# Two 64-step chunks as one 128-step unit in the HGRN2 recurrence, with the scaled state copies on ScalarE

## What is computed

```python
b = jnp.cumsum(log_f, axis=2)                       # within a chunk of 64
b_mid  = b[:, :, HG_CHUNK // 2 - 1:HG_CHUNK // 2]
b_last = b[:, :, HG_CHUNK - 1:HG_CHUNK]
scores = einsum('bnthk,bnshk->bnhts', q * exp(b - b_mid), k * exp(b_mid - b))
scores = where(causal, scores, 0.0)                 # 64 x 64
o_intra = einsum('bnhts,bnshv->bnthv', scores, iv)
q_dec, k_dec = q * exp(b), k * exp(b_last - b)
def step(state, xs):                                # one chunk after another
    o = einsum('bthk,bhkv->bthv', qc, state)
    state = dc[..., None] * state + einsum('bthk,bthv->bhkv', kc, ic)
```

## Time and profile before

| | |
|---|---|
| runs | 2416.03, 2418.9, 2420.78 us |
| median | 2418.9 us |
| span of the profiled execution, first to last instruction | 2413.7 us |
| mean granted TensorE clock | 0.979 |
| TensorE busy with matmuls | 2307.7 us (96%) |
| VectorE busy | 1268.4 us (53%) |
| ScalarE busy | 875.3 us (36%) |
| POOL busy | 146.6 us (6%) |

### The profile page before, as it was taken

One profiled execution on the slowest core, in us unless ns is written; L12 is line 12 of the kernel. 1 busy time (PEld: TensorE's weight loads), 2 busy tenths in 40 slices (PEclk: granted clock), 3 DMA queues, 4 the chain that ended last, 5 costly groups with the idle time before them and its releaser, 6 DMA issues. The chain is left out here.

```text
span 2413.7 us, 30798 instructions
## 1 busy us (share of the span) xinstructions
PE 2307.7 (96%) x11056; PEld 1867.0 (77%) x11056; DVE 1268.4 (53%) x2445; ACT 875.3 (36%) x1241; POOL 146.6 (6%) x255
## 2 busy tenths in 40 slices
PE   5899999999999999799999999979999999999997
PEld 2788888888888888688777777757877777778775
DVE  6454545454545544301556566555566565665655
ACT  6343333333333333111233323333343353354343
POOL 0000000000000000110111111110001000100100
PEclk9899999999999999899999999989999999999998
DMA  4100101010101010222222222165436535634622
GB/s 157 35 36 23 44 9 43 9 43 13 44 17 35 17 35 10 71 71 73 77 86 85 76 90 86 56 200 172 125 97 205 168 107 175 201 106 123 227 93 79
DMA packets 89269, 206.40 MB, mean 86 GB/s; under 512 B 20832, under 2 KB 30048, under 8 KB 89184
## 3 DMA queue, kind: packets, MB, share of 16 engines
q1 hardware_dynamic: 68432, 139.68, 18.3%
q0 software_dynamic: 20752, 65.57, 8.2%
HBM read 157.87 MB, written 46.14 MB: 85 GB/s over the span
## 5 line engine op out<-in xcount | busy, mean ns | idle before, releaser
L95 PE MATMUL s_ps<-u_hi,s_w_hi 128*128 128x512 f32 x768 | 305.8, 398 | 8.7 <-DVE s_w_lo L854 8.7
L96 PE MATMUL s_ps<-u_lo,s_w_hi 128*128 128x512 f32 x768 | 300.5, 391 | 0.0
L97 PE MATMUL s_ps<-u_hi,s_w_lo 128*128 128x512 f32 x768 | 299.8, 390 | 0.0
L95 PE MATMUL t_ps<-t_oa_hi,t_w_hi 128*128 128x512 f32 x512 | 204.6, 400 | 17.0 <-DVE t_oa_lo L1534 12.5
L97 PE MATMUL t_ps<-t_oa_hi,t_w_lo 128*128 128x512 f32 x512 | 202.4, 395 | 0.0
L96 PE MATMUL t_ps<-t_oa_lo,t_w_hi 128*128 128x512 f32 x512 | 202.3, 395 | 0.0
L1425 DVE TENSOR_TENSOR t_w_lo<-c_raw,t_w_hi 128x1024 fp32r<-128x1024 f32 x136 | 166.5, 1224 | 62.7 <-ACT t_w_hi L1331 62.7
L95 PEld LDWEIGHTS s_ps<-u_hi,s_w_hi 128*128 128x128 f32 x768 | 144.7, 188 | 53.1 <-issue 14.5
L97 PEld LDWEIGHTS s_ps<-u_hi,s_w_lo 128*128 128x128 f32 x768 | 144.8, 189 | 31.0
L96 PEld LDWEIGHTS s_ps<-u_lo,s_w_hi 128*128 128x128 f32 x768 | 144.8, 189 | 28.5
L1331 ACT ACTIVATE t_w_hi<-c_raw 128x1024 fp32r<-128x1024 f32 x136 | 142.5, 1048 | 42.4 <-PE t_ps L97 14.5
(11 more groups left out here) (277 smaller groups left out, 4794.3 us busy)
## 6 DMA issues: line engine op xcount, KB each, us to landing
c_raw<-w_in_in SPq DMA_DIRECT2D x56, 512.0 KB, 3.7
gates_scratch<-s_stage POOLq DMA_DIRECT2D x64, 256.0 KB, 2.7
t_ein<-gates_scratch SPq DMA_DIRECT2D x64, 256.0 KB, 4.2
c_raw<-w_o_hg_in SPq DMA_DIRECT2D x32, 512.0 KB, 5.0
c_raw<-w_out_in SPq DMA_DIRECT2D x32, 512.0 KB, 3.5
c_raw<-w_ple_gate_in SPq DMA_DIRECT2D x32, 512.0 KB, 3.5
c_raw<-w_glu_in SPq DMA_DIRECT2D x16, 512.0 KB, 3.9
t_xa<-o_gated_scratch POOLq DMA_DIRECT2D x32, 256.0 KB, 4.3
```

What stands on the lines that cost most here:

```text
L95: pe.matmul(out, w_hi, u_hi, start=first, stop=False)
L96: pe.matmul(out, w_hi, u_lo, start=False, stop=False)
L97: return pe.matmul(out, w_lo, u_hi, start=False, stop=last)
```

## The change

Two chunks of 64 steps become one unit of 128. Since a unit's scores now reach from its second half back to its first, keys and queries are kept in three forms of 64 columns a unit, ke[P, 4, 3, 64] and qe[P, 4, 3, 64]: for the keys the first half as seen from the middle of the first chunk (0), the same scaled by the decay up to the middle of the second (1), and the second half (2); for the queries the first half (0), the second as seen from the first chunk (1), and the second (2). The decay is the column coef of the second chunk. The scores of a unit are then two matmuls: 64 key columns (form 0) against 128 query columns (forms 0 and 1) into the upper 64 rows of psc, and 64 key columns (form 2) against 64 query columns (form 2) into the lower 64 rows. The lower left quarter is never written by them, so psc is set to zero once, and the mask is now the full triangle of 128.

The state is kept for 4 units instead of 8 chunks. VectorE makes G alone, with one fused instruction for a unit, and the scaled copies S come from ScalarE (`scale_states`), between the sigmoid L455 and the load of the table L456. G has two buffers. The span of a unit is the product of two coefficients and lies in R. The matrix of ones is made as F32R once and read as F32 where it was F32 (the rounded copy ones_r goes).

```diff
-            pool.wait_ge(mk, 5)
-            pool.memset(c["causal"][0:CH, CH:P], 0.0).then_inc(mk, 1)
...
-        qe = m.sb("qe", [P, TT])
-        ke = m.sb("ke", [P, TT])
+        qe = m.sb("qe", [P, NPAIR, 3, CH])
+        ke = m.sb("ke", [P, NPAIR, 3, CH])
-        S = m.sb("S", [P, NCH, P])
-        G = m.sb("G", [P, P])
+        S = m.sb("S", [P, NPAIR, P])
+        G = m.sb("G", [P, 2, P])
...
-                pe.wait_ge(qe_done, s + 1)
+                pe.wait_ge(q_far_done, s + 1)
+                pe.wait_ge(psc_zeroed, 1)
                 for p in range(NPAIR):
-                    pe.matmul(psc[:, at], ke[:, at], qe[:, at], start=True, stop=True).then_inc(turned, 1)
+                    near, both = slice(p * P + CH, (p + 1) * P), slice(p * P, (p + 1) * P)
+                    pe.matmul(psc[0:CH, both], ke[:, p, 0], qe[:, p, 0:2].rearrange("p a j -> p (a j)"), start=True, stop=True)
+                    pe.matmul(psc[CH:P, near], ke[:, p, 2], qe[:, p, 2], start=True, stop=True).then_inc(turned, 1)
 
             def outer(s):
-                for j in range(NCH):
-                    rows = slice(j % 2 * CH, j % 2 * CH + CH)
-                    out = (pk, pv)[j % 2][:, j // 2 * P:j // 2 * P + P]
-                    ins = pe.matmul(out, ken[rows, j // 2], ivn[rows, j // 2], start=True, stop=True)
+                for p in range(NPAIR):
+                    ins = pe.matmul(pk[:, p * P:(p + 1) * P], ken[:, p], ivn[:, p], start=True, stop=True)
...
             def attend(s, first):
                 for p in range(NPAIR):
-                    for j in (2 * p, 2 * p + 1):
-                        pe.wait_ge(states, s * NCH + j + 1)
-                        pe.matmul(po[:, at], S[:, j], qe[:, at], start=j % 2 == 0, stop=False, skip_group_check=True)
+                    pe.wait_ge(states, s * NPAIR + p + 1)
+                    pe.matmul(po[:, at], S[:, p], qe[:, p, 0:2].rearrange("p a j -> p (a j)"), start=True, stop=False,
+                              skip_group_check=True)
                     pe.matmul(po[:, at], ivn[:, p], sT[:, p], start=False, stop=True, skip_group_check=True).then_inc(o_done, 1)
...
+            def scale_states(s, new_head):
+                for p in range(1 if new_head else 0, NPAIR):
+                    act.wait_ge(g_done, s * NPAIR + p)
+                    act.activation(S[:, p], G[:, (p + 1) % 2], ACT.Copy, scale=coef[:, 2 * p:2 * p + 1]).then_inc(states, 1)
...
-                    dve.tensor_scalar(S[:, j], G[:], coef[:, j:j + 1], None, ALU.mult).then_inc(states, 1)
-                    dve.wait_ge(states, s * NCH + j + 1)
-                    dve.tensor_tensor(G[:], kv, S[:, j], ALU.add).then_inc(g_done, 1)
+                    dve.wait_ge(g_done, s * NPAIR + p)
+                    if p:
+                        dve.wait_ge(states, s * NPAIR + p)
+                    dve.scalar_tensor_tensor(G[:, p % 2], G[:, (p + 1) % 2], span[:, p:p + 1], kv, ALU.mult, ALU.add).then_inc(g_done, 1)
...
-                    dve.scalar_tensor_tensor(ke[:], sig[:], 1.0, b[:], ALU.subtract, ALU.mult).then_inc(ke_done, 1)
+                    dve.scalar_tensor_tensor(ke[:, :, 0], half(sig, 0), 1.0, half(b, 0), ALU.subtract, ALU.mult).then_inc(k_near_done, 1)
+                    dve.scalar_tensor_tensor(ke[:, :, 2], half(sig, 1), 1.0, half(b, 1), ALU.subtract, ALU.mult).then_inc(ke_done, 1)
+                    dve.tensor_tensor(ke[:, :, 1], ke[:, :, 0], second, ALU.mult).then_inc(k_far_done, 1)
+                    dve.tensor_tensor(span, coef[:, 0:NCH:2], coef[:, 1:NCH:2], ALU.mult).then_inc(span_done, 1)
...
-                    dve.scalar_tensor_tensor(qe[:], pq[:], c["nomlb"][:, ds(h, 1)], lf[:], ALU.mult, ALU.mult).then_inc(qe_done, 1)
+                    dve.scalar_tensor_tensor(qe[:, :, 2], half(pq, 1), c["nomlb"][:, ds(h, 1)], half(lf, 1), ALU.mult, ALU.mult
+                    dve.scalar_tensor_tensor(qe[:, :, 0], half(pq, 0), c["nomlb"][:, ds(h, 1)], half(lf, 0), ALU.mult, ALU.mult
+                    dve.tensor_tensor(qe[:, :, 1], qe[:, :, 2], second, ALU.mult).then_inc(q_far_done, 1)
...
+            dve.memset(psc[:], 0.0).then_inc(psc_zeroed, 1)
-            act.activation(ones_r[:], c["ones"][:], ACT.Copy).then_inc(ones_done, 1)
```

More of the change, by code:

```diff
@@ L152, in _ @@
         def _(pool):
-            pool.memset(c["ones"][:], 1.0).then_inc(ones_done, 1)
+            pool.memset(c["ones"][:].bitcast(F32), 1.0).then_inc(ones_done, 1)
             pool.memset(c["ident"][:], 0.0).then_inc(mk, 1)
@@ L172, in _ @@
                 pe.wait_ge(sq_done, n + 1)
-                pe.matmul(ms[:, t], c["ones"][:], sq[:, n % 2], start=k == 0, stop=k == KT - 1).then_inc(ms_done, 1)
+                pe.matmul(ms[:, t], c["ones"][:].bitcast(F32), sq[:, n % 2], start=k == 0, stop=k == KT - 1).then_inc(ms_done, 1)
         @block.scalar
@@ L480, in _ @@
             turned_iv(STEPS - 1)
+            scale_states(STEPS - 1, False)
             norm(STEPS - 1, False)
@@ L487, in _ @@
             chunks = lambda x: x[:].rearrange("p (n j) -> p n j", j=CH)
+            half = lambda x, i: x[:].rearrange("p (a b j) -> p a b j", b=2, j=CH)[:, :, i]
+            second = coef[:].rearrange("p (a b) -> p a b", b=2)[:, :, 1:2].to_broadcast([P, NPAIR, CH])
             col = lambda x: x.rearrange("p (n a) -> p n a", a=1)
@@ L499, in turned_scores, with carry_state @@
                                     psc[:].rearrange("p (a n) -> p a n", a=NPAIR)).then_inc(masked, 1)
-            def carry_state(s, new_head):
+            def carry_state(s, new_head, first):
                 dve.wait_ge(kv_done, s + 1)
-                for j in range(NCH):
-                    kv = (pk, pv)[j % 2][:, j // 2 * P:j // 2 * P + P]
-                    if new_head and j == 0:
+                dve.wait_ge(span_done, s + 1)
+                if not first:
+                    dve.wait_ge(states, s * NPAIR)
+                for p in range(NPAIR):
+                    kv = pk[:, p * P:(p + 1) * P]
+                    if new_head and p == 0:
                         dve.memset(S[:, 0], 0.0).then_inc(states, 1)
-                        dve.wait_ge(states, s * NCH + 1)
-                        dve.tensor_copy(G[:], kv).then_inc(g_done, 1)
+                        dve.tensor_copy(G[:, 0], kv).then_inc(g_done, 1)
                         continue
-                    if j == 0:
-                        dve.wait_ge(coef_done, s + 1)
-                    dve.wait_ge(g_done, s * NCH + j)
-                    dve.tensor_scalar(S[:, j], G[:], coef[:, j:j + 1], None, ALU.mult).then_inc(states, 1)
-                    dve.wait_ge(states, s * NCH + j + 1)
-                    dve.tensor_tensor(G[:], kv, S[:, j], ALU.add).then_inc(g_done, 1)
+                    dve.wait_ge(g_done, s * NPAIR + p)
+                    if p:
+                        dve.wait_ge(states, s * NPAIR + p)
+                    dve.scalar_tensor_tensor(G[:, p % 2], G[:, (p + 1) % 2], span[:, p:p + 1], kv, ALU.mult, ALU.add).then_inc(g_done, 1)
             def split_square(s):
@@ L544, in head @@
                         turned_scores(n - 1)
-                        carry_state(n - 1, t == 1)
+                        carry_state(n - 1, t == 1, first and t == 1)
                     dve.wait_ge(sigg, n + 1)
@@ L555, in head @@
                     dve.wait_ge(r_done, 2 * n + 2)
+                    if recur:
+                        dve.wait_ge(states, n * NPAIR)
                     dve.tensor_tensor(col(coef[:]), col(R[:, 0:NCH]), mids, ALU.add).then_inc(arg_done, 1)
@@ L1286, in mean_square @@
                     pe.wait_ge(ln_done, use)
-                pe.matmul(ms[which][:], c["ones"][:], sumsq[:], start=True, stop=True).then_inc(ms_done, 1)
+                pe.matmul(ms[which][:], c["ones"][:].bitcast(F32), sumsq[:], start=True, stop=True).then_inc(ms_done, 1)
             def unit(sec, t, body, u, i, first, last):
@@ L1558, in build @@
                  omlb=m.sb("omlb", [P, HEADS]), nomlb=m.sb("nomlb", [P, HEADS]), eps=m.sb("eps", [P, 1]),
-                 ones=m.sb("ones", [P, P]), ident=m.sb("ident", [P, P]), causal=m.sb("causal", [P, P]),
+                 ones=m.sb("ones", [P, P], F32R), ident=m.sb("ident", [P, P]), causal=m.sb("causal", [P, P]),
                  restart=m.sb("restart", [P, TT]), raw=m.sb("raw", [P, 2, KT, P]),
```

33 lines of the change are left out of this document (20 added, 13 removed).

## The result

The changed kernel took 2379.38 us in the median of four runs (2373.46 to 2382.14), the kernel before in the same job 2417.47 us (2413.72 to 2420.78). The ratio is 0.9836, with a 95% interval of 0.9816 to 0.9855: faster, by 38 to 40 us (35 to 44 by the interval). The forecast was 2386 us and a gain of 33.3 us, its range began at 2379. The ratio times the median of this job is 2377.8 us, times that of the first three runs 2379.2 us: the direction is as forecast and the gain lies at or past the very end of the range.

A forecast was written before the change was run, and what follows sets the result against it. The HGRN2 phase was taken as bound by TensorE's queue of matmul passes. Covered steps -29.1, last step -4.0 and start -0.2 sum to -33.3 us, from 2418.9 to 2386 us; range 2379 to 2391, widened to 2400.

The forecast's parts named there:

- the work on VectorE and ScalarE in the covered steps: Shorter sums and longer ke, qe and copies in the 31 steps covered by projections: costed at nothing, hidden behind projections.
- The price of passes and halves: On TensorE: a pass costs 0.112 us even at half the columns; halves of columns cost 0.33, of rows 0.39.
- `attend`, -0.90 us a step: State product and scores in `attend`: 8 passes fewer at 0.112 us each, 0.90 us less a step.
- `outer`, -0.39: Outer products: 8 whole-array passes replace 16 on 64 rows, 1.36 us instead of 1.75, 0.39 less a step.
- `turn`, +0.35: Score matmuls: 16 passes on column halves side by side instead of 8 whole-array ones, 0.35 us more a step.
- Rival 2: In `turn`, score halves run one after the other: 0.45 us more a step, 14 us worse, 2400 us; chance 0.08.
- Rival 3: In the scores, weight loads lie bare: 0.90 us a step on top, 5.4 us gained, 2413 us; chance 0.03.
- Rival 4: In the scores, each change between halves pays: 1.56 us instead of 0.35, no overlap, 2437 us, slower; chance 0.02.
- The covered steps, -29.1 us: The 31 HGRN2 steps covered by projections: -0.90 - 0.39 + 0.35 = -0.94 us each, -29.1 us in all.
- The last step, -4.0 us: The 32nd HGRN2 step, uncovered: a shorter chain of sums and copies gains 4.0 us, bounds 3.3 and 4.5.
- The start, -0.2 us: Before the first weights on ScalarE: the rounded copy of the ones, 0.31 us, goes; 0.2 us counted as gained.
- 2 us for all that lies outside the phase: Later phases do not change and only start earlier; their waits for DMA can give or take 2 us.

The follow-up runs named there:

- e6: Changed kernel with the scaled copies of the state back on VectorE, inside its chain of sums; 2381.0 us, ratio 0.9849.
- e1: Changed kernel with `attend`'s product with the state as two float32 matmuls of 64 query columns on the same weights; 2409.8 us, ratio 0.9966.
- e3: Changed kernel with the four upper score matmuls first and the four lower behind them, instead of in turns; 2384.3 us, ratio 0.9862.
- e4: Changed kernel with outer products by 64 rows again, odd chunks' sums left out of the state (for time alone); 2392.8 us, ratio 0.9900.
- e2: Changed kernel with one score matmul a unit on the whole array (scores false, for time alone); 2369.6 us, ratio 0.9796.
- e5: Kernel before, 8 chunks kept, with only fused sums on VectorE and scaled copies on ScalarE; 2413.7 us, ratio 0.9987.
- e9: Changed kernel, unchanged, with more runs and a second profile; 2377.6 us, ratio 0.9840.
- e7: Changed kernel with the unit as one chunk of 128, one form of keys and queries, one whole-array score matmul; 2369.5 us, ratio 0.9799.

## Why the prediction was right, and where it was not

**The step that failed.** The forecast was 33.3 us, the runs gained 38 to 40. Two terms were put at nothing and were not nothing: the work on VectorE and ScalarE in the covered steps (1.0 us) and the time from the last mean square to S5 (0.46 us). The gain of the three groups of TensorE came out 1.0 us larger in all, that of the last step 0.3 smaller. The rest, 2 to 4 us, lies outside the phase, where the prediction allowed 2 us. Its cause is only in part known. The price of passes and halves, which makes most of the gain, was right.

**What bounds.** Right: the phase is a queue of TensorE passes, and it remained one at a clock of 1.00. The score passes of both halves started together, no wait of TensorE came up in the covered steps, and moving the copies between VectorE and ScalarE in the changed kernel (e6) changed them by nothing.

**`attend`, -0.90 us a step.** Measured -0.894 (3.137 to 2.243), and e1 shows the reason: passes, not columns. The prediction said that such a pass costs what its weight load costs; the 0.058 and 0.11 us of e3 for 64 weight columns agree with a price by the larger of the two sides, weights or streamed columns. That is inferred from the shapes in these traces.

**`outer`, -0.39.** Measured -0.398, shown by e4.

**`turn`, +0.35.** Measured +0.32, shown by e2. Rival 2 (halves one after the other) is out by the rows of the changed kernel; e3 gives only 0.08 of its 0.45 even in the order that should bring it about. Rival 3 is out: with bare weight loads `turn` would be 0.9 us longer still. For column halves on all 128 rows the trace does not bear out the sentence of the Trainium skill ("TensorE: Matmul & The Clock Gate", "Part 3: Packing small matmuls") that loads overlap only for a different row group: 16 passes, each with its load, fit into the time of 8 and 0.32 us. Rival 4 is out with them.

**The covered steps, -29.1 us.** The three groups give 31 x 0.971 = -30.1. The mean square's wait, 1.0 us in all, went as well. This is the step that failed in kind: "Work that leaves or joins VectorE and ScalarE in the 31 is worth nothing by itself." I had read the waits of TensorE's matmuls; this one stands in the rows of its weight loads and in the starts alone. e5 takes it away with the shorter chain on VectorE alone, and it stays away in e6, where the copies are back in that chain.

**The last step, -4.0 us.** Measured -3.67, since a scaled copy takes 0.40 us. But another 0.46 us came between it and S5, and that term was missing. Before, the granted clock fell inside the last step: 0.79 in the mean from 962 to 976 us, 0.50 after that. The changed kernel's last step, shorter and denser, ran at 1.00 from 931.5 to 941.5:

```profile
931.50:941.50 10.00, 5.96 (x52) 4.96 (x50) 5.94 (x12) 4.51 (x9) 0.54 (x1) 1.00 0.07 26
```

The second pass of its mean square came 0.34 us behind the first (941.58 to 941.92) instead of 0.59 (975.75 to 976.34), and ScalarE's next instruction came 0.78 us behind the first (942.36) instead of 1.25 (977.00). That is the 0.46; from there to S5 both take 8.7 us. e5 has it too, with a last step of 11.66 us. The clock fell ahead of the last mean square in both traces of the kernel before and behind it in all the others, but in e6 it had also fallen once inside the last step. That the shorter step keeps it up is likely, not shown.

**The start, -0.2 us.** Not to be seen: the first projection began anywhere from 67.2 to 72.0 us over eleven traces.

**The sum.** -30.1 - 1.0 - 3.7 - 0.5 = -35.3 us, where the two profiles have 916.4 and 880.7 us for the phase, -35.7. The forecast had -33.1 for it. Of the 2.6 us between them, 1.5 are the terms left out, 1.0 the groups of the covered steps; the last step takes 0.3 back, and 0.4 is left over. The 0.4 lies in the projections behind `outer`: from their second matmul to their last they take 0.015 us less in each step (5.01 us before, 5.00 after). What remains of the 38 to 40 us, 2 to 4, lies outside the phase. There S5 scatters by 1.6 us and the tail by 8.6 us among kernels that are the same there.

Both go with the granted clock. S5 starts at 0.50 in every trace, and a projection matmul steps by 0.43 us until the clock is back at 1.00, then by 0.23. That came 5.0 us after the first matmul of S5 before, 3.0 after the change (first row before, second after; columns as in the earlier trace rows):

```profile
985.68:990.70 5.02, 5.02 (x12) 4.00 (x13) 0.17 (x1) 0.22 (x1) 0.00 (x0) 0.50 0.59 160
954.10:959.00 4.90, 4.90 (x23) 4.02 (x23) 3.13 (x10) 1.93 (x3) 0.00 (x0) 1.00 0.34 111
```

The 2.0 us between them, at 0.43 us a matmul instead of 0.23, cost 0.9 us, and 0.9 is the difference between 608.1 and 607.2. Over all the traces it came after 2.9 to 6.1 us, and S5 is longer in the same order, but for 0.2 us. In the tail the stretches at 0.50 add up to 38.8 us in the shortest one (813.6), to 41 to 43 us in the four of 816.1 to 817.4, and to 48 to 54 us in the six of 818.4 to 822.2.

Is any of it the change's? Each interval of the ratio reaches down to 35 us, so neither of the two measurements alone tells 39 from 36. But take the gain of the medians over the kernel before, and subtract what the phase gains in the traces (from 916.4 us before). In all eight measurements of the changed form, 1.4 to 4.3 us remain; in e5, whose groups are those of before, nothing. With the second profile before (917.3 us) each is 0.9 us less. So a surplus that comes with the changed form is likely. The clock at the start of S5 gives 0.9 us of it in six of the eight; e4 and e6 had it back no sooner than the kernel before. e9 was meant to tell and did not: its ratio repeats the first, while its S5 and tail are 0.8 and 2.6 us shorter than those of the first profile before, and 1.3 and 0.1 shorter than those of the second. Where the rest of the surplus lies stays open.

**The range.** With 2 us for all that lies outside the phase, its lower end sat on the measured value. It was also narrower than its own bounds. With 0.4 for `outer` and only 0.1 for `turn` the step gains 0.90 + 0.40 - 0.10 = 1.20 us, not 1.1, and the range would begin at 2375.

## What to carry to other kernels

On 128 weight columns count float32 passes, not streamed columns: two matmuls of 64 columns on the same weights cost twice one of 128. With 64 weight columns this no longer holds (0.058 us for 64 streamed columns, 0.11 for 128, in e3). A group on halves of the array paid 0.3 to 0.4 us here over the same work on the whole array, and eight pairs of passes did not win it back. Look first for an algebraic form that fits the whole array: e7 beat the use of halves. And before calling an engine free, look at the waits of the weight loads and at the starts, in the iteration that carries extra work, not in a typical one. When phases that did not change differ between two profiles, compare their granted clocks before their code.

## What was not expected of the hardware

- TensorE does not start all its matmuls in the order written: a half of the array takes its passes ahead of those written earlier for the other half. In the changed kernel the eighth lower pass started before the last two upper ones; in e3 the first lower one started 0.5 us behind the first upper one, past three that stand ahead of it.
- A pass with 64 weight columns steps by 0.11 us for 128 streamed columns and by 0.058 us for 64 (e3); with 128 weight columns, 64 streamed columns cost 0.112 us.
- Eight pairs of passes of 64 rows took no less time than eight passes of 128 rows, and 0.40 us more with the way in and out (e4).
- A copy of 128x128 float32 on ScalarE with a scale from memory takes 0.40 us (mean of 120), the plain copy of that size, from float32 to float32r, 0.31 us in the one instance there is the earlier trace rows.
- The tail phase varied between 813.6 and 822.2 us with no change in it, and with it the time at the half clock, from 38.8 to 53.9 us.
